# Attention of a fused two-block kernel: mask and suffix sums added onto the scores in PSUM, heads started earlier in four banks, and the convolution's taps placed at other points

## The chip, the cores and the metric

The program runs on one core of a Trainium2 chip. Its engines are TensorE (PE, matrix products, with its weight loads PEld), VectorE (DVE), ScalarE (ACT), GpSimd (POOL) and the queue SP, which issues the weight transfers. The metric is device time in microseconds, lower is better: 1041.95 us before, the median of three runs (1041.51 to 1042.3).

## The reference, cut to what matters

256 tokens of width 1024 pass through two blocks. The first (a convolution and gating mixer, 32 experts with routing, a gated projection, a final norm) isn't touched. The second begins with a norm, one wide projection `w_in_2` and three branches:

```python
h = rmsnorm_2(x, norm_mix_pre)
proj = h @ w_in                 # conv_in 1024, q 512, k 512, v 512, g_conv 1024, g_att 1024 columns
u = glu(conv_in)                                # 512 channels
u = causal_depthwise_conv(u, conv_dw_w, conv_dw_b)      # 31 taps per channel
conv_out = silu(layernorm_2(u)) @ w_conv_branch + b_conv_branch
# 8 heads of 64, two query blocks of 128:
z = einsum('bqhd,bkhd->bhqk', qb, kb) / 8
mask = s_idx < t_idx
log_1m = where(mask, log_sigmoid(-z), 0)
rev_excl = reverse_cumsum(log_1m) - log_1m
a = where(mask, exp(log_sigmoid(z) + rev_excl), 0)
att = einsum('bhqk,bkhd->bqhd', a, vb)
merged = sigmoid(g_conv) * conv_out + sigmoid(g_att) * (att @ w_att_branch)
```

A residual sum with `merged @ w_out` and a feed-forward part of width 2816 follow. Since log_sigmoid(z) equals z minus softplus(z) and log_sigmoid(-z) equals minus softplus(z), the exponent of a key s is z(s) minus the sum of softplus over all keys from s on.

## The kernel before, in words

**Data.** Tokens lie along the free axis (256 of them), channels along the 128 partitions. Each fp32 weight is used as two rounded parts: ACT writes `wh` = round(w) (`split_hi`, L259), DVE writes `wl` = w - wh (`split_lo`, L266), each in pieces of 128x1024, eight of which fit in WH and WL. Activations are in two parts as well. A product of 128 columns (`three`) is 24 matmuls of 256 columns: eight with wh and the high part, eight with wh and the low part, eight with wl. `wide` gives V with tokens on the partitions: 24 matmuls of 512 columns for each half. Piece i may be written when the product of piece i-8 is done (`freed_by`).

**Order.** It is written out by hand for each engine, and engines meet in semaphores (`Sig`): each engine runs strictly through its own list. `w_in_2` is nine groups of four pieces: group 0 and 1 the convolution's input, 2 is Q, 3 is K, 4 is V, and 5 to 8 the 16 gate products.

- `in2_pe` computes groups 0 to 4; before V two transposes (L1492) turn a row of scales into a column (`RC`).
- `in2_dve` copies products out of PSUM times the norm's scale (L1533 and L1540 for the convolution's input, L1546 for Q, L1553 for K), splits `wl`, and puts taps of the depthwise convolution between: 93 `scalar_tensor_tensor` for channel groups 0 to 2 (`taps_dve`, L1457; the first of each group is L1454). Six taps follow each Q and K copy, 13 the group of V. Eight multiplications of the residual (L1529, `x4`) stand ahead of the first copy.
- The fourth channel group is scaled by ACT (`taps_act`, L1466) and added by POOL (`att_pool`, L1689), 30 times each.
- `att_pe`, `att_dve`, `att_act` hold the attention and the 16 gate products, two gates to a head (one for head 0), in turns s = 0 to 8. For a head: `scores` (PE, two fp32 products of K and Q); DVE scales them and adds the mask into SBUF (`ZM`, L1630); ACT takes |z|, exp(-|z|) and ln(1 + .) (L1665, L1667, L1669); DVE adds max(z, 0) (L1634), which is softplus; `suffix` (PE, a triangular and an all-one matrix into another bank); DVE subtracts it from ZM (L1641); ACT takes exp (L1675); `values` (PE) multiplies with V. Scores use banks 2 and 3, suffix sums 4 and 5, values 6 and 7, gates 0 and 1. DVE copies each gate out at L1621, and the next gate but one waits for that (`sg_in`). ATH and ATL (L1681, L1647) are the two parts of the attention's output.
- `merge_*` begins with the mean over the convolution's result, which needs every tap and the last gate's copy.

Of the kernel before, what the change touches and what calls it, by code (L numbers as in the profile page):

```python
# [31 lines left out]
C_ID, C_U, C_TRI, C_NM, C_IOTA, C_IX, C_SLOT = 0, 128, 256, 384, 768, 832, 840  # L32
N_CST = 841
# [65 lines left out]
def build(nc, dr, out_ap):  # L99
    ctx = ExitStack()  # L100
    with ctx:
# [38 lines left out]
        tri = cst[:, C_TRI:C_TRI + 128]  # L140
        nm = cst[:, C_NM:C_NM + 384]
# [1265 lines left out]
        ZM = A(11384, 2, 384)  # L1407
        AB = A(o + 4608, 2, 384)
# [3 lines left out]
        TP = A(19712, 4, 256)  # L1412
        IN2 = n_piece[("in2", 0), 0]
# [11 lines left out]
        vv = sig("vv", range(2))  # L1425
        tap_v = sig("tap_v", [(3, 0)] + [(j, k) for k in range(31) for j in range(3)])
# [5 lines left out]
        s_zm = sig("zm", range(8))  # L1432
# [4 lines left out]
        s_c2 = sig("c2", range(8))  # L1437
# [30 lines left out]

        def in2_pe(e):
# [19 lines left out]
            e.wait_ge(*r45.at(0))  # L1489
            e.wait_ge(*q_.at(2))  # L1490
            for i in range(2):
                k = e.transpose(ps[2][:, i * 128:i * 128 + 128], R45[:, i * 128:i * 128 + 128], ident)  # L1492
            k.then_inc(*rcol.up("turned"))
            for i in range(2):
                wide(e, ps[i][:, :], "in2", 4, i, H5H, H5L)

        def in2_act(e):
# [12 lines left out]
            split_hi(e, IN2 + 16 + 8)  # L1510
# [4 lines left out]
            split_hi(e, IN2 + 16 + 10)  # L1515

        def in2_dve(e):
# [10 lines left out]
            for c in range(8):  # L1528
                e.tensor_tensor(XT[:, c, :], XN[:, c, :], RB[:, 1, :], M).then_inc(*x4.up(c))  # L1529
# [14 lines left out]
            for j in range(4):  # L1544
                e.wait_ge(*proj.at("in2", 2, j))
                e.tensor_tensor(QT[:, j, :], ps[j][:, 0:256], R45, M).then_inc(*q_.up(j))  # L1546
                if j == 0:
                    e.tensor_scalar(CA[:, 3, :], CU[:, 3, 0:256], dw(3, 0), vcol("dw_b", 3), M, ADD).then_inc(*tap_v.up(3, 0))
                taps_dve(e, 6)
                split_lo(e, IN2 + 8 + j + 7)  # L1550
            for j in range(4):
                e.wait_ge(*proj.at("in2", 3, j))
                e.tensor_tensor(KT[:, j, :], ps[4 + j][:, 0:256], R45, M).then_inc(*k_.up(j))  # L1553
                taps_dve(e, 6)
                split_lo(e, IN2 + 12 + j + 7)
            e.wait_ge(*rcol.at("turned"))
            e.tensor_copy(RC, ps[2][:, 0:256].rearrange("p (i n) -> p i n", i=2)[:, :, 0]).then_inc(*rc.up(0))
            split_lo(e, IN2 + 16 + 10)
            taps_dve(e, 13)

        def att_pe(e):
            def scores(h):
                b, r, j = 2 + h % 2, 64 * (h % 2), h // 2
                if h < 2:
                    e.wait_ge(*(rc.at(0) if h == 0 else q_.at(3)))
                    e.wait_ge(*k_.at(3))
                else:
                    e.wait_ge(*s_zm.at(h - 2))
                mm(e, ps[b][:, 0:256], KT[r:r + 64, j, 0:128], QT[r:r + 64, j, :], True, True)
                mm(e, ps[b][:, 256:384], KT[r:r + 64, j, 128:256], QT[r:r + 64, j, 128:256], True,  # L1570
                   True).then_inc(*s_sc.up(h))

            def suffix(h):
                b, x = 4 + h % 2, AB[:, h % 2, :]
                e.wait_ge(*s_sp.at(h))
                if h >= 2:
                    e.wait_ge(*s_c2.at(h - 2))
                mm(e, ps[b][:, 0:256], tri, x[:, 0:256], True, False)
                mm(e, ps[b][:, 128:256], one, x[:, 256:384], False, True)
                mm(e, ps[b][:, 256:384], tri, x[:, 256:384], True, True).then_inc(*s_suf.up(h))  # L1580

            def values(h):
                b, r, x = 6 + (h // 2) % 2, 64 * (h % 2), AB[:, h % 2, :]
                e.wait_ge(*s_at.at(h))
                if h == 0:
                    e.wait_ge(*vv.at(1))
# [627 lines left out]
```

## Time and profile before

| | |
|---|---|
| median of three runs | 1041.95 us |
| the profiled execution | 1045.19 us, its span 1043.5 us |
| PE / DVE / ACT / POOL busy | 957.3 / 505.4 / 330.3 / 32.3 us |
| mean granted TensorE clock | 0.968 |
| stage from 642.5 to 778.9 us of the span | second block's Q, K, V, attention, gates |

Times below are microseconds from the start of the span. In a timeline row the first number is the start, the second the time that the row covers, `xN` the number of instructions merged in it, and the bracket the idle time before it and the instruction that ended it. Merged rows overlap a little with the next, so steps are read from start to start. PEclk 1.00 is 2.4 GHz and 0.50 is 1.2 GHz. An fp32 product shows as two matmul records.

### The profile page before, as it was taken

Reading aid. Unit: us, or ns where it says so; the run is one execution under the profiler, and the core shown is the slowest. Engines: PE = TensorE matmul, PEld = TensorE weight load, DVE = VectorE, ACT = ScalarE, POOL = GpSimd, SP = SyncE. Lnnn points to the kernel's source line nnn. Section 1 sums busy time; section 2 is a strip of 40 time slices with the busy share of each in tenths; the row PEclk is TensorE's granted clock in tenths of the full one; section 3 lists DMA queues with packets and bytes.
Section 4 is the critical chain, followed back from the end, with each engine's and each line's share of the span. In section 5 each row is a group of like instructions: output and inputs, shape, how many; then the busy total and the mean of one; then the engine's idle time right before and its main releaser. Section 6 shows DMA issues by size and latency. Waiting matters only on the chain.

```text
span 1043.5 us, 14199 instructions
## 1 busy us (share of the span) xinstructions
PE 957.3 (92%) x5910; PEld 681.7 (65%) x5910; DVE 505.4 (48%) x886; ACT 330.3 (32%) x523; POOL 32.3 (3%) x39
## 2 busy tenths in 40 slices
PE   5999799999999999998989799778888989999997
PEld 5997535443434444443434788768778979999885
DVE  5684513122322222222312676986777657766742
ACT  4723211101000000100001554425557645554541
POOL 1000000000000000000000000012420000000000
PEclk9999799999999999999999899988999989999999
DMA  9947699999999999999999522442422533545401
GB/s 359 409 187 291 272 376 416 421 430 430 430 430 430 431 431 429 430 430 431 430 428 428 221 81 82 162 161 81 143 100 82 193 151 105 219 162 180 184 1 40
DMA packets 23621, 289.52 MB, mean 277 GB/s; under 512 B 2560, under 2 KB 4864, under 8 KB 6016
## 3 DMA queue, kind: packets, MB, share of 16 engines
q1 hardware_dynamic: 22832, 286.98, 67.4%
q10 hardware_dynamic: 720, 1.57, 0.4%
q8 instruction: 49, 0.80, 0.3%
q14 instruction: 20, 0.16, 0.0%
HBM read 287.49 MB, written 1.05 MB: 277 GB/s over the span
## 4 chain that ended last, share of the span: by engine, by line
PE 71%; DVE 14%; ACT 6%; DMA 5%; issue 4%; SPq 0%; DVEq 0%; ACTq 0%
PE ps L270 70%; DVE wl L266 5%; DMA ring<-in_moe 4%; DVE arena L1457 3%; ACT wh L259 2%; DMA ring<-in_w_in 1%; PE ps L959 1%; ACT arena L1466 0%; DVE arena L547 0%; DVE arena L1634 0%; DVE arena L352 0%; DVE arena L1641 0%; ACT arena L1665 0%; ACT arena L1669 0%; ACT arena L1667 0%
## 5 line engine op out<-in xcount | busy, mean ns | idle before, releaser
L270 PE MATMUL ps<-ring,arena 128*64 128x512 f32 x1232 | 341.5, 598 | 8.6 <-issue 8.5
L270 PEld LDWEIGHTS ps<-ring,arena 128*64 128x64 f32 x1232 | 109.5, 138 | 170.1 <-issue 167.9
L266 DVE TENSOR_TENSOR wl<-ring,wh 128x1024 fp32r<-128x1024 f32 x150 | 180.2, 1231 | 63.3 <-ACT wh L259 63.2
L270 PE MATMUL ps<-arena 128*64 128x512 f32 (+5 forms) x432 | 163.3, 533 | 13.2 <-ACT arena L1675 11.6
L259 ACT ACTIVATE wh<-ring 128x1024 fp32r<-128x1024 f32 x150 | 150.8, 1049 | 33.1 <-PE ps L270 29.7
L1070 DVE SCALAR_TENSOR_TENSOR arena<-ps,arena 128x512 f32<-128x512 f32 x16 | 12.0, 750 | 216.5 <-PE ps L270 216.5
L270 PEld LDWEIGHTS ps<-arena 128*64 128x64 f32 (+2 forms) x432 | 59.1, 149 | 61.4 <-issue 44.3
L270 PE MATMUL ps<-up_h,wh 128*128 128x256 f32 x352 | 88.3, 286 | 4.6 <-DVE up_l L1866 4.6
L270 PE MATMUL ps<-up_l,wh 128*128 128x256 f32 x352 | 87.8, 285 | 0.0
L270 PE MATMUL ps<-h_h,wh 128*128 128x256 f32 x256 | 69.2, 302 | 5.0 <-DVE wl L266 2.5
L270 PEld LDWEIGHTS ps<-up_h,wh 128*128 128x128 f32 x352 | 67.5, 192 | 4.9 <-issue 4.9
L1143 ACT ACTIVATE y_h<-ps 128x512 fp32r<-128x512 f32 x32 | 19.1, 597 | 158.5 <-PE ps L270 158.5
L270 PEld LDWEIGHTS ps<-up_l,wh 128*128 128x128 f32 x352 | 67.5, 192 | 0.0
L270 PE MATMUL ps<-h_l,wh 128*128 128x256 f32 x256 | 66.9, 293 | 0.0
L1084 DVE TENSOR_TENSOR arena<-arena,ps 128x512 f32<-128x512 f32 x64 | 40.9, 680 | 41.7 <-PE ps L270 41.7
L270 PEld LDWEIGHTS ps<-h_h,wh 128*128 128x128 f32 x256 | 51.2, 200 | 6.9 <-issue 4.1
L270 PE MATMUL ps<-up_h,wl 128*128 128x256 f32 x352 | 54.7, 285 | 0.0
L270 PEld LDWEIGHTS ps<-h_l,wh 128*128 128x128 f32 x256 | 51.2, 200 | 0.0
L1076 DVE TENSOR_TENSOR y_l<-ps,y_h 128x512 fp32r<-128x512 f32 x32 | 22.0, 687 | 59.2 <-ACT y_h L1143 59.2
L1136 ACT ACTIVATE arena<-ps 128x512 f32<-128x512 f32 x16 | 9.6, 597 | 128.4 <-PE ps L959 128.4
L1689 POOL TENSOR_TENSOR arena<-arena 128x256 f32<-128x256 f32 x30 | 27.3, 910 | 718.5 <-ACT arena L1466 716.1
L270 PEld LDWEIGHTS ps<-up_h,wl 128*128 128x128 f32 x352 | 48.0, 192 | 0.0
(260 smaller groups left out, 1531.1 us busy)
## 6 DMA issues: line engine op xcount, KB each, us to landing
ring<-in_moe SPq DMA_DIRECT2D x77, 2048.0 KB, 22.1
arena<-in_moe SPq DMA_DIRECT2D x19, 2048.0 KB, 26.6
ring<-in_w_in SPq DMA_DIRECT2D x12, 2048.0 KB, 8.8
ring<-in_w_up SPq DMA_DIRECT2D x11, 2048.0 KB, 7.7
ring<-in_w_dn SPq DMA_DIRECT2D x5, 2048.0 KB, 7.8
ring<-in_w_out SPq DMA_DIRECT2D x4, 2048.0 KB, 14.9
ring<-in_w_pg SPq DMA_DIRECT2D x2, 2048.0 KB, 21.5
ring<-in_w_in SPq DMA_DIRECT2D x2, 1024.0 KB, 10.4
```

Of the source, the lines that this page charges most:

```text
L259: e.activation(wh(i), raw_piece(i), ACT.Copy).then_inc(*hi.up(i))
L266: e.tensor_tensor(wl(i), raw_piece(i), wh(i), SUB).then_inc(*lo.up(i))
L270: return e.matmul(o, l, r, start=first, stop=final, skip_group_check=True)
L959: k = e.transpose(ps[4][:, f * 128:f * 128 + 128], HD[:, f * 128:f * 128 + 128], ident)
L1070: e.scalar_tensor_tensor(out=HD, in0=ps[1][:, :], scalar=RW[:, q % 2, 1:2], in1=HD, op0=M, op1=M).then_inc(*hid.up(q))
L1076: e.tensor_tensor(l[:, :], ps[5 + n][:, :], h[:, :], SUB).then_inc(*yl.up(q, n))
L1084: e.tensor_tensor(x, x, ps[ZB[z]][:, :], ADD).then_inc(*acc.up(q, z))
L1136: e.activation(HT.rearrange("p a b -> p (a b)"), ps[4][:, :], ACT.Copy).then_inc(*b4.up(q))
L1143: e.activation(parted(q, n)[0][:, :], ps[5 + n][:, :], ACT.Copy).then_inc(*yh.up(q, n))
L1457: e.scalar_tensor_tensor(out=CA[:, j, :], in0=src, scalar=dw(j, k), in1=CA[:, j, :], op0=M, op1=ADD).then_inc(*tap_v.up(j, k))
L1689: e.tensor_tensor(CA[:, 3, :], CA[:, 3, :], TP[:, k % 4, :], ADD).then_inc(*tap_p.up(k))
```

## The change

**Scores.** Q is scaled by 0.125 when it is copied out. The mask is added on PE: a product of the identity and the mask, both rounded (`IDR`, `NMR`, two new ACT copies), goes onto the scores' bank, once for each masked square, two per head. ACT reads |z| from PSUM. `suffix` multiplies with -1 matrices and accumulates onto the same bank, and ACT's last exp reads PSUM. L1630 and L1641, eight instructions each on DVE, are gone, and so is ZM. A head keeps one of the banks 2 to 5 from its scores to its last exp, and one of four AB buffers.

**Order.** Heads 0 to 3 get their scores within groups 3 and 4, heads 0 and 1 their suffix sums too; the rest stand one by one between the gates. ACT takes softplus of heads 0 to 3 and exp of 0 and 1 in `in2_act`. The eight residual multiplications go behind group 4's splits. Taps: three for each Q copy and for each K copy but the last, and behind the split; 12 around the first heads; four for each of the first 15 gates. ACT's taps begin during Q, where its splits for pieces 14 on now wait behind `tap_v` (3, 0), DVE's first instruction on channel group 3.

The core of the diff (ACT's and DVE's parts of a head become the helpers `softplus_act`, `softplus_dve` and `weights_act`):

```diff
+        def scores(e, h):
+            b, r, j = 2 + h % 4, 64 * (h % 2), h // 2
+            e.wait_ge(*k_.at(j))
+            if h == 0:
+                for x in range(2):
+                    e.wait_ge(*masks.at(x))
+            elif h == 2:
+                e.wait_ge(*rc.at(0))
+            elif h >= 4:
+                e.wait_ge(*s_at.at(h - 4))
+            mm(e, ps[b][:, 0:256], KT[r:r + 64, j, 0:128], QT[r:r + 64, j, :], True, False)
+            mm(e, ps[b][:, 0:128], IDR[:, :], NMR[:, :], False, False)
+            mm(e, ps[b][:, 256:384], KT[r:r + 64, j, 128:256], QT[r:r + 64, j, 128:256], False, False)
+            mm(e, ps[b][:, 256:384], IDR[:, :], NMR[:, :], False, False).then_inc(*s_sc.up(h))
...
 in2_pe:
+                if j in (1, 2):
+                    scores(e, j - 1)
...
+            suffix(e, 0)
+            wide(e, ps[0][:, :], "in2", 4, 0, H5H, H5L)
+            suffix(e, 1)
+            scores(e, 2)
+            wide(e, ps[1][:, :], "in2", 4, 1, H5H, H5L)
+            scores(e, 3)
...
 in2_act:
+            e.wait_ge(*tap_v.at(3, 0))
+            for j in range(8):
+                split_hi(e, IN2 + 15 + j)
+                taps_act(e, 1)
+                if j == 6:
+                    softplus_act(e, 0)
+            softplus_act(e, 1)
...
 in2_dve:
             split_lo(e, IN2 + 10)
-            for c in range(8):
-                e.tensor_tensor(XT[:, c, :], XN[:, c, :], RB[:, 1, :], M).then_inc(*x4.up(c))
...
-                taps_dve(e, 6)
                 split_lo(e, IN2 + 8 + j + 7)
+                taps_dve(e, 3)
...
+            softplus_dve(e, 0)
...
 att_pe:
+            for g in range(16):
...
+                if g in (1, 3, 5, 7):
+                    scores(e, 4 + g // 2)
+                if g in (0, 2, 4, 6, 8, 10):
+                    suffix(e, 2 + g // 2)
+                if g in (0, 1, 2, 4, 6, 8, 10, 12):
+                    values(e, (0, 1, 2, 4, 6, 8, 10, 12).index(g))
```

DVE's list around Q and the first K copy, before (`proj`: the product is done; `hi`: the piece of wh is there):

```order
L1546 TENSOR_TENSOR arena<-ps1,arena 128x256 [waits proj]
L1457 SCALAR_TENSOR_TENSOR arena<-arena,vec 128x256 [waits tap_v] x6
L266 TENSOR_TENSOR wl_51<-ring,wh_50 128x1024 [waits hi]
L1546 TENSOR_TENSOR arena<-ps2,arena 128x256 [waits proj]
L1457 SCALAR_TENSOR_TENSOR arena<-arena,vec 128x256 [waits tap_v] x6
```

The same place in the changed kernel, to the first K copy (L1625 copies Q, L1453 and L1456 are taps, L1633 copies K):

```order
L1625 SCALAR_TENSOR_TENSOR arena<-ps0,arena 128x256 [waits proj,cpad,glu]
L1628 TENSOR_SCALAR arena<-arena,vec 128x256
L266 TENSOR_TENSOR wl_51<-ring,wh_50 128x1024 [waits hi]
L1453 TENSOR_SCALAR arena<-arena,vec 128x256 x3
L1625 SCALAR_TENSOR_TENSOR arena<-ps1,arena 128x256 [waits proj]
L266 TENSOR_TENSOR wl_51<-ring,wh_50 128x1024 [waits hi]
L1456 SCALAR_TENSOR_TENSOR arena<-arena,vec 128x256 [waits tap_v] x3
L1625 SCALAR_TENSOR_TENSOR arena<-ps2,arena 128x256 [waits proj]
```

Three taps stand where six stood, behind the split and not ahead of it.

PE's list in group 3 in the changed kernel, with what is added there (`+`) between the second and the third K product:

```order
 L270 MATMUL ps5<-h5_h_65,wl_51 128x256 x7
+L270 MATMUL ps2<-arena 128x256 [waits masks,k]
+L270 MATMUL ps2<-nm_r_70,id_r_69 128x128
+L270 MATMUL ps2<-arena 128x128
+L270 MATMUL ps2<-nm_r_70,id_r_69 128x128
 L270 MATMUL ps6<-h5_h_65,wh_50 128x256 [waits hi,glu]
```

Head 0's scores wait for the first K copy, and the third K product, which needed only `hi` and `glu`, now stands behind that wait.

DVE's list between two gates, before:

```order
L1641 TENSOR_TENSOR arena<-arena,ps5 128x384 [waits suffix]
L1457 SCALAR_TENSOR_TENSOR arena<-arena,vec 128x256 [waits tap_v] x2
L1621 TENSOR_TENSOR arena<-ps0,arena 128x256 [waits proj]
L266 TENSOR_TENSOR wl_51<-ring,wh_50 128x1024 [waits hi]
L1457 SCALAR_TENSOR_TENSOR arena<-arena,vec 128x256 [waits tap_v] x2
L1630 SCALAR_TENSOR_TENSOR arena<-ps2,cst 128x384 [waits c2,scores]
```

and in the changed kernel (L1669 copies a gate, L1519 is the softplus sum of a head):

```order
L1669 TENSOR_TENSOR arena<-ps1,arena 128x256 [waits proj]
L266 TENSOR_TENSOR wl_51<-ring,wh_50 128x1024 [waits hi]
L1456 SCALAR_TENSOR_TENSOR arena<-arena,vec 128x256 [waits tap_v] x4
L1519 SCALAR_TENSOR_TENSOR arena<-ps2,arena 128x384 [waits ln]
L1669 TENSOR_TENSOR arena<-ps0,arena 128x256 [waits proj]
```

Both DVE steps that waited for a head's products are gone from between the gates, and a gate has four taps there.

## Rows read from the trace of the kernel before

**Rows 1.** Which engines were busy (the page, part 1; share of the span)

```profile
PE 957.3 (92%) x5910; PEld 681.7 (65%) x5910; DVE 505.4 (48%) x886; ACT 330.3 (32%) x523; POOL 32.3 (3%) x39
```

**Rows 2.** Busy time, PEclk, DMA share and GB/s in three stretches, all engines

```profile
642.50:668.00 25.50, 23.20 (x193) 23.02 (x194) 22.03 (x47) 15.74 (x18) 0.00 (x0) 1.00 0.47 167
668.00:701.10 33.10, 21.21 (x107) 17.35 (x105) 30.04 (x61) 6.62 (x10) 0.24 (x1) 0.89 0.43 164
701.10:778.90 77.80, 66.23 (x441) 59.76 (x441) 55.73 (x88) 42.49 (x77) 27.05 (x30) 0.92 0.30 109
```

**Rows 3.** Who PE waited for from 640 to 780 (total, times, longest)

```profile
PE ps L270 <- ACT arena L1675: 11.6, 7, 2.8
PE ps L270 <- DVE wl L266: 7.5, 1, 7.5
PE ps L270 <- DVE arena L1634: 4.4, 1, 4.4
PE ps L270 <- DVE arena L1533: 1.6, 1, 1.6
PE ps L270 <- ACT wh L259: 0.7, 1, 0.7
```

**Rows 4.** PE's timeline: V, a head with a gate, the stage's end

```profile
679.58 3.75 PE L270 MATMUL ps<-wl,h_h 128*128 128x512 f32 x8 [7.55 <-DVE wl L266]
...
683.13 0.48 PE L270 MATMUL ps<-wh,h_h 128*128 128x512 f32 x1
...
688.91 0.92 PE L270 MATMUL ps<-arena 64*128 64x256 f32 x4
...
741.76 1.71 PE L270 MATMUL ps<-arena 128*64 128x256 f32 x8 [1.80 <-ACT arena L1675]
...
743.41 0.39 PE L270 MATMUL ps<-h_h,wh 128*128 128x256 f32 x1
...
746.36 0.59 PE L270 MATMUL ps<-arena,cst 128*128 128x256 f32 x2
...
747.16 0.37 PE L270 MATMUL ps<-h_h,wh 128*128 128x256 f32 x1
...
752.04 1.71 PE L270 MATMUL ps<-arena 128*64 128x256 f32 x8 [1.79 <-ACT arena L1675]
...
778.87 1.99 PE L270 MATMUL ps<-arena,ones 128*128 128x256 f32 x8
```

**Rows 5.** DVE's timeline: residual, first Q copy, six taps, a split

```profile
640.97 2.76 DVE L1529 TENSOR_TENSOR arena<-arena 128x256 f32<-128x256 f32 x8
...
656.19 0.42 DVE L1546 TENSOR_TENSOR arena<-ps,arena 128x256 f32<-128x256 f32 x1
...
660.48 2.45 DVE L1457 SCALAR_TENSOR_TENSOR arena<-arena,vec 128x256 f32<-128x256 f32 x6
...
662.85 1.21 DVE L266 TENSOR_TENSOR wl<-ring,wh 128x1024 fp32r<-128x1024 f32 x1
...
663.99 0.41 DVE L1546 TENSOR_TENSOR arena<-ps,arena 128x256 f32<-128x256 f32 x1
```

**Rows 6.** ACT's timeline: ten splits, and one step of softplus

```profile
649.55 9.60 ACT L259 ACTIVATE wh<-ring 128x1024 fp32r<-128x1024 f32 x10
...
747.13 0.53 ACT L1665 ACTIVATE arena<-arena 128x384 f32<-128x384 f32 x1 [2.60 <-DVE arena L1630]
```

**Rows 7.** PE alone in short stretches: busy, PEclk, DMA share, GB/s

```profile
672.00:676.00 4.00, 0.04 (x1) 1.00 0.00 0
680.00:683.00 3.00, 3.00 (x8) 0.50 0.91 279
711.00:717.00 6.00, 6.00 (x23) 0.50 0.77 317
```

**Rows 8.** Timelines of DVE (two taps) and POOL (four additions)

```profile
734.51 1.83 DVE L1457 SCALAR_TENSOR_TENSOR arena<-arena,vec 128x256 f32<-128x256 f32 x2
731.90 4.16 POOL L1689 TENSOR_TENSOR arena<-arena 128x256 f32<-128x256 f32 x4 [6.12 <-ACT arena L1466]
```

More of the change, by code:

```diff
@@ L1412, in build @@
         TP = A(19712, 4, 256)
+        IDR, NMR = rounded("id_r", 20736, 128), rounded("nm_r", 20864, 128)
         IN2 = n_piece[("in2", 0), 0]
@@ L1469, in in2_pe, with weights_act @@
+        def weights_act(e, h):
+            e.wait_ge(*s_suf.at(h))
+            e.activation(AB[h % 4], ps[2 + h % 4][:, 0:384], ACT.Exp).then_inc(*s_at.up(h))
         def in2_pe(e):
@@ L1599, in gates @@
                 three(e, ps[j % 2][:, 0:256], "in2", 5 + n, j, H5H, H5L)
-            for s in range(9):
-                if s < 8:
-                    scores(s)
-                if 1 <= s < 8:
-                    gates()
-                if s >= 1:
-                    suffix(s - 1)
-                gates()
-                if s >= 1:
-                    values(s - 1)
+                if g in (1, 3, 5, 7):
+                    scores(e, 4 + g // 2)
+                if g in (0, 2, 4, 6, 8, 10):
+                    suffix(e, 2 + g // 2)
@@ new lines, in rest @@
+            def rest(j):
+                e.wait_ge(*at_h.at(j))
+                e.tensor_tensor(ATL[:, j, :], ps[6 + j % 2][:, 0:256], ATH[:, j, :], SUB).then_inc(*at_l.up(j))
+            for g in range(16):
+                if g:
+                    gate(g - 1)
+                split_lo(e, IN2 + 20 + g + 7)
+                if g in (3, 6, 10, 14):
+                    rest((3, 6, 10, 14).index(g))
+                if g == 0:
+                    softplus_dve(e, 3)
+                taps_dve(e, 4)
+                if g in (2, 4, 6, 8):
+                    softplus_dve(e, 3 + g // 2)
@@ new lines, in rounded_part @@
+            def rounded_part(j):
+                e.wait_ge(*s_val.at(2 * j + 1))
+                e.activation(ATH[:, j, :], ps[6 + j % 2][:, 0:256], ACT.Copy).then_inc(*at_h.up(j))
+            for g in range(16):
+                if g in (1, 3, 5, 7, 9, 11):
+                    weights_act(e, 2 + g // 2)
+                if g in (2, 4, 6, 8):
+                    softplus_act(e, 3 + g // 2)
+                if g in (2, 5, 9, 13):
+                    rounded_part((2, 5, 9, 13).index(g))
+                split_hi(e, IN2 + 20 + g + 7)
+                taps_act(e, 1)
```

186 lines of the change are left out of this document (72 added, 114 removed).

## Prediction

> **What bounds the kernel now.** I read the page first. PE is busy 92% of the span [rows 1], and a change to it that saves no matmuls can pay only where PE waits or runs slowly. Second, the busy time by stretch [rows 2]: in the stage that the change touches, from 642.5 to 778.9, PE is busy 110.6 of 136.4 us, by a measure that counts slow matmuls as busy, and the granted clock is below full in the last two stretches (0.89, 0.92). DVE is busy 22.0 of 25.5, then 30.0 of 33.1, then 55.7 of 77.8 us. So DVE is nearly full until the heads begin and has room after that. Third, PE's waits [rows 3]: 7.5 us for the low parts of V's weights, 4.4 for the first softplus, 11.6 in seven waits for a head's last exp, 1.6 for the first copy behind the residual's products, and 0.7 for a split. Last, the timelines, for the steps of a turn.
>
> The steady turn is one head and two gates. It takes 752.04 - 741.76 = 10.28 us [rows 4]. Of it PE needs 1.65 for values and the next scores (741.76 to 743.41), 2.95 from there to the next suffix sum, 0.80 for that (746.36 to 747.16), and some 2.9 for the other gate: 8.2 to 8.3, and 1.8 is the wait. I use 2.85 for a product of 24 matmuls (0.119 each), 0.83 each for scores and values, 0.80 for suffix sums. Half of V takes 688.91 - 683.13 = 5.78. The wait ends a ring through DVE and ACT: mask, three ACT steps of 0.53 [rows 6], sum, suffix sums, subtraction, exp. DVE's own work does not fill a turn.
>
> **The change part by part.** All in the time of the profiled execution (1045.19 us, 3.2 above the median of the runs shown).
>
> *Residual moved.* Eight DVE products, 2.7 us [rows 5], leave the head of the copies. What follows on DVE and ACT (copies, sigmoids, splits) is 2.7 earlier: the first Q copy at 656.19 - 2.7 = 653.5. PE's waits of 1.6 and 0.7 go.
>
> *When PE reaches head 0's scores.* PE began its long wait at 679.58 - 7.55 = 672.0, after 16 matmuls of V (3.9) and two short transposes: group 3 ended near 668.0. Less 2.3 it is 665.7, and the second K product, two products earlier, ends at 660.0.
>
> *When DVE gives it K.* Between the first Q copy and the end of the first K copy DVE has four Q copies (0.35 to 0.41, so 1.5), one scaling (0.4), four splits of 663.99 - 662.85 = 1.14 (4.6), twelve taps of 2.37 / 6 = 0.395 (4.7) and the K copy (0.35): 11.6 us. Two things come on top. ACT's splits now stand behind `tap_v`; ACT is free of it at 654.3, a split takes 0.96 [rows 6], and DVE waits 1.0. Queued behind that wait on ACT are all later splits, which it then makes at 1.4 with a tap each, faster than DVE uses them. And POOL's additions now begin during Q, six of them by then. Beside two additions two taps take 1.83 instead of 0.79 [rows 8], 0.5 for each addition: 3.0. Bounds: nothing, if they fall on instructions that POOL does not disturb; POOL's whole 27.05 / 30 = 0.9 [rows 2], so 5.4. I take 0.5, the row for the same pair of operations. Sum 15.6: K is there at 669.1, and **PE waits 9 us** where it waited 7.5 later on. This is the price of the early scores: products 3 and 4 of K queue behind them. The clock goes low in such a wait: it did in the wait of 7.5 us, and was at 1.2 GHz until 683 after PE resumed at 679.6 [rows 4, 7]. I charge 1.8 us, half of that time.
>
> *To the first gate.* Mask products: 16 in all, of 128 columns, not in this trace. Not above 0.20 (a quarter of a suffix sum, by fp32 columns), not below nothing; nearest is a rounded matmul of 256 columns, 0.119, and I take 0.12, so 1.07 for scores. From 669.1: scores, K, scores, K (7.8) and 1.8 for the clock, 678.7. DVE then needs the last K copy, a split and the softplus sum (2.0): suffix sums start at 680.7. Suffix, V, suffix, scores, V, scores: 0.8 + 5.8 + 0.8 + 1.1 + 5.8 + 1.1 = 15.3, and the first gate starts at 696.0. The low parts of V have long been split by then, so the wait of 7.5 goes, and so does the one of 4.4.
>
> *The gates.* PE: 16 x 2.85 + 6 x 0.80 + 8 x 0.83 + 4 x 1.07 = 61.3, ending at 757.3 if nothing holds it. DVE: 18 splits (20.5), 60 taps (23.7), 17 additions of POOL beside it (8.5), 16 copies (5.9), five softplus sums and four low parts (4.0, at about 0.45, between a copy and ACT's 0.53): 62.6. It can begin when ACT has done softplus of head 3 (1.6) and a split (1.0) after PE's 696.0, at 698.6, so it ends at 761.2. The two run within 4 us of each other over 16 gates, and each gate has about one gate's time of slack (a gate waits for the copy two before). Exp, softplus and splits on ACT are some 2.5 us a gate, with room; a head's exp is a gate ahead of its values, so the 11.6 us go. Taps are not removed anywhere: DVE loses 16 instructions of 384 columns (8.5 us at ACT's 0.53 for the same size), and takes on nearly as much by POOL's additions, of which four began 2.6 us before DVE's pair of taps in [rows 8] and now find DVE at work. That is why DVE, and not PE, ends the stage.
>
> *The sum.* The mean over the convolution starts at 761.2 and not at 778.87 [rows 4]: -17.7 us. What follows has the same instructions and the same order, and weights are no limit: transfers take 0.47, 0.43 and 0.30 of these stretches [rows 2]. 1045.19 - 17.7 = 1027.5, against the median 1041.95 - 17.7 = **1024.3**.
>
> On POOL and DVE the trace shows 0.5 us lost by DVE for an addition. The Trainium skill, SBUF — State Buffer, section "SBUF: two separate sides", says that the port pair they share is an exclusive lock, and that the loser is blocked for the whole instruction. The sum above goes by the row; by the rule, with DVE always the loser, it would be the third case below. The row agrees in kind, since both engines slow down (POOL 1.04 an addition in [rows 8]), and not in that size.
>
> **The rivals.**
>
> *PE ends the stage (additions cost DVE little).* Then K comes 3.0 earlier, the first gate starts at 693.0, PE ends at 754.3 and the last copy at 754.7: -24.2, 1017.8. For it: splits and PSUM copies may be undisturbed, and they are a third of DVE's time. Against it: 1.83 for two taps.
>
> *DVE pays 0.9 for each addition.* 6 x 0.4 more before K and 17 x 0.4 in the gates: 9.2, which leaves -8.5, 1033.5. For it: DVE has almost no idle time now for POOL to run in. Against it: no row has DVE paying in full.
>
> *The heads don't run ahead.* If one in-order queue still ties each head's exp to the gate before it, two gates keep 10.28: 696.0 + 8 x 10.28 = 778.2, no change, 1041.3. For it: ACT waits in order for suffix sums ahead of splits. Against it: softplus of heads 0 to 3 is done before the first gate.
>
> *Slower: the clock stays low.* The mechanism is the wait for K: if PE goes to 1.2 GHz there and further waits keep it there through the gates, a gate with its part of the heads, 61.3 / 16 = 3.83 at full clock, takes up to twice that; V's last eight matmuls show 3.55 / 8 = 0.44 for 512 columns at the low level (679.58 to 683.13 [rows 4]) against 0.24, so 1.8 times, 3.05 more a gate. PE may end 778.87 - 757.3 = 21.6 later before the gain is gone: that is seven gates. With all 16 it is 48.8 - 21.6 = 27 later than before, 1069. For it: in this trace the clock was low again from 711 to 717. Against it: that followed waits of 4.4 and 2.8 us close together, and later waits of 1.8 in every turn left it at 2.4 GHz; the gates should have none above 1.
>
> **How the numbers follow.** The forecast 0.60, with 1018 to 1030 as its own range; PE ends the stage 0.15; additions in full 0.13; no running ahead 0.07; clock low 0.05. The time is that of the forecast, 1024. The range takes in the second and third case: 1014 to 1034. A change under 0.2% (2.1 us) can't be told from none here. Faster is the first three and a part of the fourth, 0.90; same 0.05; slower 0.05.
>
> **What would show it.** PE waits about 9 us between the second and the third K product, for K's copy, with the clock low for 3 to 4 us after it; a wait near 2 before head 0's suffix sums; no wait for V's low parts; from the first gate to the mean some 65 us, DVE busy over 90% of it, and taps there at 0.5 or more on average; PE's waits in the gates for the copy of a gate and not for exp. I am wrong if PE waits in the gates for exp or suffix sums, if the clock falls there, or if the part after the attention changes in length by more than 2 us.

## The result, and the profile after

| | before | after |
|---|---|---|
| median of the runs side by side | 1041.73 us (1040.66 to 1042.3) | 1030.09 us (1027.85 to 1033.81) |
| the profiled execution / its span | 1045.19 / 1043.5 us | 1029.13 / 1027.4 us |
| mean granted clock | 0.968 | 0.973 |

The ratio is 0.9893, with a 95% interval of 0.9861 to 0.9925: the change is faster by 1.1%, which is clear of the noise but less than 2%. The forecast was 1024, its range 1014 to 1034.

The two profiled executions differ by 16.1 us, more than the medians do. About 5 us of that belong to neither order of the attention: in the profile of before the stage begins at 630.80, in that of after at 625.85, and what stands ahead of it (the first block) is the same code. Over the fourteen profiles of this study that start lies anywhere between 625.9 and 630.8. So I measure the **stage**: from DVE's first reciprocal of the second norm to PE's first product of the mean over the convolution. It holds all that the change touches. Waits inside it repeat to 0.01 us between kernels that share the code up to them, and what follows it takes 263.5 to 265.8 us in every profile. What doesn't repeat is where TensorE's clock is low behind a wait; the section on the experiments says what that comes to.

| | start | mean starts | stage | rest |
|---|---|---|---|---|
| before | 630.80 | 778.87 | 148.07 | 264.6 |
| after | 625.85 | 762.66 | 136.81 | 264.7 |

The stage is 11.3 us shorter; 17.7 were forecast. 11.3 agrees with the medians (11.6).

The page of after, part 1, answers to [rows 1]. PE's share of the span rose by a point, since the same products and the 16 for the mask stand in less time:

```profile
PE 955.8 (93%) x5926; PEld 679.4 (66%) x5926; DVE 499.5 (49%) x870; ACT 329.9 (32%) x525; POOL 37.8 (4%) x39
```

Busy time in three stretches of after (columns as in [rows 2]): to the end of the wait for K, from there to the first gate, and from the first gate to the mean:

```profile
637.50:663.70 26.20, 17.25 (x145) 16.95 (x143) 22.09 (x38) 15.98 (x23) 5.30 (x6) 0.88 0.54 208
663.70:694.10 30.40, 28.49 (x134) 22.91 (x135) 22.10 (x42) 12.61 (x23) 9.03 (x7) 0.88 0.38 139
694.10:762.60 68.50, 65.79 (x477) 58.86 (x477) 59.97 (x103) 37.17 (x61) 18.31 (x17) 1.00 0.33 123
```

The reader is to see where PE now has holes: 9 us in the first stretch, 1.9 in the second, 2.7 in the last. In the last one PE is busy 65.79 of 68.5 us at full clock, while DVE is busy 59.97, but that isn't spread evenly. DVE alone over the last 27.6 us of the stage, and two rows of its timeline there:

```profile
735.00:762.60 27.60, 27.60 (x47) 1.00 0.40 153
```

```profile
753.82 3.60 DVE L1456 SCALAR_TENSOR_TENSOR arena<-arena,vec 128x256 f32<-128x256 f32 x4
757.34 0.41 DVE L1669 TENSOR_TENSOR arena<-ps,arena 128x256 f32<-128x256 f32 x1
```

DVE has no hole there; four taps took 3.60 us beside four of POOL's additions, where 1.66 is usual. PE's last two waits (1.03 at 757.81 and 1.74 at 762.66) are for its copies of gates. Who PE waited for from 636 to 766 in after answers to [rows 3]:

```profile
PE ps L270 <- DVE arena L1633: 9.0, 1, 9.0
PE ps L270 <- DVE arena L1669: 2.8, 2, 1.7
PE ps L270 <- DVE arena L1519: 1.9, 1, 1.9
```

The waits of 11.6, 7.5, 4.4, 1.6 and 0.7 us are gone, 25.8 in all, and 13.7 took their place. The timeline of PE in after shows the three places, and two steps of a turn:

```profile
663.71 1.22 PE L270 MATMUL ps<-arena 64*128 64x256 f32 x2 [8.96 <-DVE arena L1633]
...
677.91 1.14 PE L270 MATMUL ps<-arena,cst 128*128 128x256 f32 x6 [1.90 <-DVE arena L1519]
...
685.44 0.70 PE L270 MATMUL ps<-arena 64*128 64x256 f32 x2
...
686.07 0.33 PE L270 MATMUL ps<-nm_r,id_r 128*128 128x128 f32 x1
...
686.33 0.48 PE L270 MATMUL ps<-arena 64*128 64x128 f32 x2
...
686.74 0.33 PE L270 MATMUL ps<-nm_r,id_r 128*128 128x128 f32 x1
...
686.90 0.45 PE L270 MATMUL ps<-wh,h_h 128*128 128x512 f32 x1
...
694.11 0.33 PE L270 MATMUL ps<-h_h,wh 128*128 128x256 f32 x1
...
708.91 0.39 PE L270 MATMUL ps<-h_h,wh 128*128 128x256 f32 x1
...
718.08 0.39 PE L270 MATMUL ps<-h_h,wh 128*128 128x256 f32 x1
```

A head's scores with its two mask products take 686.90 - 685.44 = 1.46 us. Two gates with one head take 718.08 - 708.91 = 9.17, where they took 10.28 [rows 4]. PE alone behind the wait for K (busy, PEclk, DMA share, GB/s) answers to [rows 7]:

```profile
664.00:671.00 7.00, 7.00 (x29) 0.51 0.40 122
672.00:676.00 4.00, 4.00 (x30) 1.00 0.49 209
```

Through 7 us of unbroken work the granted clock is 1.2 GHz, and 2.4 GHz from 670.8 on, 7.1 us after PE resumed. DVE's timeline around the first Q copy and the K copy, which answers to [rows 5]:

```profile
648.56 0.42 DVE L1625 SCALAR_TENSOR_TENSOR arena<-ps,arena 128x256 f32<-128x256 f32 x1
...
653.30 1.69 DVE L266 TENSOR_TENSOR wl<-ring,wh 128x1024 fp32r<-128x1024 f32 x1
...
654.91 2.21 DVE L1456 SCALAR_TENSOR_TENSOR arena<-arena,vec 128x256 f32<-128x256 f32 x3
...
662.06 1.26 DVE L1456 SCALAR_TENSOR_TENSOR arena<-arena,vec 128x256 f32<-128x256 f32 x3
663.25 0.41 DVE L1633 TENSOR_TENSOR arena<-ps,arena 128x256 f32<-128x256 f32 x1
```

Three taps take 1.26 us alone and 2.21 beside POOL's additions, a split 1.69 instead of 1.21.

### The profile page after: what moved, and what is told of

It reads as the page before. It is cut to its first block, busy times and chain, and to the rows that moved or that the text cites. A ratio compares the mean times of both kernels' runs of the same rounds, so it can differ in the third digit from the quotient of the medians.

```text
span 1027.4 us, 14198 instructions
## 1 busy us (share of the span) xinstructions
PE 955.8 (93%) x5926; PEld 679.4 (66%) x5926; DVE 499.5 (49%) x870; ACT 329.9 (32%) x525; POOL 37.8 (4%) x39
## 4 chain that ended last, share of the span: by engine, by line
PE 77%; DVE 11%; DMA 4%; ACT 4%; issue 3%; SPq 0%; DVEq 0%; ACTq 0%
PE ps L270 76%; DVE wl L266 4%; DMA arena<-in_moe 4%; DVE arena L1456 2%; ACT wh L259 1%; PE ps L959 1%; DMA vec<-in_vec 0%; DVE arena L547 0%; DVE arena L352 0%; ACT arena L1762 0%; ACT in_h L617 0%; DVE arena L1084 0%; DVE arena L1669 0%; DVE arena L1805 0%; ACT arena L1765 0%
## 5 line engine op out<-in xcount | busy, mean ns | idle before, releaser
L270 PE MATMUL ps<-arena 128*64 128x512 f32 (+4 forms) x432 | 163.9, 530 | 10.6 <-DVE arena L1633 9.0
L1709 POOL TENSOR_TENSOR arena<-arena 128x256 f32<-128x256 f32 x30 | 32.6, 1088 | 695.8 <-ACT arena L1465 694.7
```

The costliest lines, as they stand in the source:

```text
L270: return e.matmul(o, l, r, start=first, stop=final, skip_group_check=True)
L1709: e.tensor_tensor(CA[:, 3, :], CA[:, 3, :], TP[:, k % 4, :], ADD).then_inc(*tap_p.up(k))
```

## Experiments

I compare by the stage, since the medians carry the changing start as well. The ratio is against before.

| kernel | median us (lowest to highest) | ratio, 95% interval | stage |
|---|---|---|---|
| after | 1030.09 (1027.85 to 1033.81) | 0.9893, 0.9861 to 0.9925 | 136.81 |
| sums_only | 1027.77 (1026.7 to 1030.43) | 0.9868, 0.9849 to 0.9887 | 134.18 |
| warm | 1028.77 (1026.44 to 1032.34) | 0.9886, 0.9861 to 0.991 | 133.71 |
| q_taps_later | 1025.76 (1022.11 to 1027.9) | 0.9839, 0.9817 to 0.9861 | 131.86 |
| mask_out | 1026.83 (1025.08 to 1027.97) | 0.9861, 0.9841 to 0.9881 | 131.02 |
| mask_one | 1026.22 (1025.29 to 1027.98) | 0.9868, 0.9849 to 0.9887 | 132.24 |
| mask_twice | 1027.08 (1024.5 to 1028.36) | 0.985, 0.9818 to 0.9881 | 132.87 |
| split_first | 1028.59 (1026.12 to 1031.04) | 0.9885, 0.9864 to 0.9905 | 137.27 |
| act_taps_later | 1027.81 (1027.18 to 1028.26) | 0.9851, 0.9815 to 0.9887 | 134.15 |
| residual_back | 1034.77 (1032.38 to 1035.24) | 0.9914, 0.9886 to 0.9942 | 141.50 |
| best1 | 1020.09 (1017.59 to 1021.06) | 0.9793, 0.9776 to 0.981 | 126.90 |
| old_order_tuned | 1015.4 (1013.8 to 1017.98) | 0.9754, 0.9737 to 0.9771 | 119.71 |
| old_order_tuned2 | 1013.87 (1013.55 to 1014.28) | 0.9719, 0.9689 to 0.9749 | 120.31 |

Each stage is read from one profile, and the clock in it varies. Here the stage of the kernels in the new order is cut at head 0's scores (K is there) and at the first gate. The fifth column is PE's work at 1.2 GHz behind the wait for K; the last says whether the clock fell again behind the wait of 1.90 us for head 0's softplus sum, which all ten have.

| kernel | K there | K to first gate | first gate to mean | low clock behind K | falls again |
|---|---|---|---|---|---|
| after | 37.86 | 30.40 | 68.55 | 7.1 | no |
| warm | 37.89 | 27.28 | 68.54 | none | no |
| q_taps_later | 31.52 | 31.84 | 68.50 | 6.8 | yes |
| mask_out | 37.86 | 26.97 | 66.19 | 4.5 | no |
| mask_one | 37.86 | 27.69 | 66.69 | 4.8 | no |
| mask_twice | 37.85 | 27.74 | 67.28 | 3.9 | no |
| split_first | 37.87 | 32.33 | 67.07 | 7.9 | yes |
| act_taps_later | 35.11 | 30.50 | 68.54 | 7.3 | no |
| residual_back | 40.54 | 32.42 | 68.54 | 8.1 | yes |
| best1 | 31.54 | 30.17 | 65.19 | 6.7 | yes |

The lists of after and split_first are the same up to head 0's suffix sums, and yet the clock fell behind the wait of 1.90 in one and not in the other. A row of PE's timeline and PE alone in split_first, to set beside the row at 677.91 above, which took 1.14:

```profile
680.33 1.90 PE L270 MATMUL ps<-arena,cst 128*128 128x256 f32 x6 [1.90 <-DVE arena L1519]
```

```profile
680.00:683.00 3.00, 2.67 (x9) 0.59 0.00 0
```

That second fall, with a longer first one, puts the first gate 1.93 us later. So a difference of up to 2 us between two stages, if it lies between K and the first gate, is not the edit's. Why the clock fell in one execution and not in the other is open.

### sums_only: the new sums in the old order

Before, with one part of the change alone: mask and suffix sums accumulate on the scores' bank. Two banks, the old turns, all taps and the residual stay where they were.

```diff
-                mm(e, ps[b][:, 0:256], KT[...], QT[...], True, True)
-                mm(e, ps[b][:, 256:384], KT[...], QT[...], True, True).then_inc(*s_sc.up(h))
+                mm(e, ps[b][:, 0:256], KT[...], QT[...], True, False)
+                mm(e, ps[b][:, 0:128], IDR[:, :], NMR[:, :], False, False)
+                mm(e, ps[b][:, 256:384], KT[...], QT[...], False, False)
+                mm(e, ps[b][:, 256:384], IDR[:, :], NMR[:, :], False, False).then_inc(*s_sc.up(h))
...
-                b, x = 4 + h % 2, AB[:, h % 2, :]
+                b, x = 2 + h % 2, AB[:, h % 2, :]
```

> The kernel before with the arithmetic of the change alone: the mask added by the identity product and the suffix sums accumulated onto the scores in PSUM, in the old order, the old two banks, and with the old places of the taps and the residual. Theory: a turn of one head and two gates (10.28 us before) is a ring, and the ring loses two DVE steps on either side of ACT (0.5 + 0.5 us) while PE gains two mask products (0.6), so a turn takes 9.6 to 10.0 and the whole -2 to -5 us against before (about 1038). V's wait of 7.5 us stays. Rival (the order alone brings the gain, the arithmetic nothing): 1041 to 1042. Rival (the arithmetic brings most of it): 1033 or less.

Measured: stage 134.18, so -13.9 from before, 2.6 better than the whole change. What I expected failed by 8.9 us at least, and the rival that gave the arithmetic most of the gain (1033 or less) held: 1027.77. PE's waits from 636 to 766 in this kernel:

```profile
PE ps L270 <- DVE wl L266: 7.5, 1, 7.5
PE ps L270 <- DVE arena L1633: 2.3, 1, 2.3
PE ps L270 <- DVE arena L1536: 1.7, 1, 1.7
PE ps L270 <- ACT wh L259: 0.7, 1, 0.7
```

There is no wait for an exp: the 11.6 us of [rows 3] are gone without any head running ahead. A turn, read on DVE's softplus sums of two heads, is 726.55 - 717.58 = 8.97 us:

```profile
717.58 0.56 DVE L1633 SCALAR_TENSOR_TENSOR arena<-ps,arena 128x384 f32<-128x384 f32 x1 [0.45 <-ACT arena L1664]
...
726.55 0.56 DVE L1633 SCALAR_TENSOR_TENSOR arena<-ps,arena 128x384 f32<-128x384 f32 x1 [1.05 <-ACT arena L1664]
```

PE alone from 700 to 720, in before and then in sums_only:

```profile
700.00:720.00 20.00, 16.06 (x75) 0.66 0.29 105
```

```profile
700.00:720.00 20.00, 20.00 (x138) 0.93 0.28 106
```

So a part of the gain is the clock. Before worked 16.6 us at 1.2 GHz, behind its waits of 7.5, 4.4 and 2.8; sums_only 7.1, behind 7.5 and 2.3. By the price that warm shows below (3.1 for 7.1 us) the 9.5 us are worth some 4, an estimate, and PE's waits fell by 13.6; the mask products take some 4.5 of it back.

So the arithmetic carries the gain. The new order as a whole added nothing to it: it swapped V's wait of 7.5 for K's of 9.0, and its stage is 2.6 longer. Whether it really costs that much isn't shown, with one profile of each and run times that overlap (1026.7 to 1030.43 against 1027.85 to 1033.81).

### warm: PE kept at work in the wait for K

72 products into an unused bank, of operands that are there, ahead of head 0's scores. Nothing waits for them.

```diff
+                if j == 1:
+                    e.wait_ge(*glu.at(3))
+                    for _ in range(72):
+                        mm(e, ps[7][:, 0:256], H5H[:, 0, 0:128], H5H[:, 0, :], True, True)
                 if j in (1, 2):
                     scores(e, j - 1)
```

> The changed kernel with 72 idle matmuls of 256 columns (their output is never read) put on PE between the second K product and head 0's scores, where it waits 9 us for K. They should end about when K comes. Theory: the wait costs a second time through the clock, which stayed at 1.2 GHz for 7.7 us after it; with PE kept busy the clock stays at 2.4 GHz and the time falls by 3 to 4 us, less what DVE then holds back, so -2 to -4 against the changed kernel (about 1027), and its runs agree within 1 us of each other where they spread over 6. Rival (DVE sets the end, the clock costs nothing): 1030, no change. Rival (the spread of 6 us comes from elsewhere): the spread stays.

Measured: stage -3.1. PE's timeline, then PE alone in two stretches (columns as in [rows 7]):

```profile
655.29 8.79 PE L270 MATMUL ps<-h_h 128*128 128x256 f32 x72
664.43 0.70 PE L270 MATMUL ps<-arena 64*128 64x256 f32 x2 [0.35 <-DVE arena L1637]
```

```profile
658.00:664.00 6.00, 6.00 (x51) 1.00 0.67 284
664.00:671.00 7.00, 6.65 (x43) 1.00 0.27 75
```

43 matmuls in the 7 us in which after made 29. The low clock behind the wait costs 3.1 us, not the 1.8 that I charged. (It lasted 7.1 us in after; the 7.7 that I expected from was misread.) The spread of the run times stayed at 6 us, where I had expected 1, so the clock in this place is not what makes the runs differ.

### q_taps_later: the taps between the Q copies moved behind the group

```diff
                 split_lo(e, IN2 + 8 + j + 7)
-                taps_dve(e, 3)
...
             split_lo(e, IN2 + 24)
+            taps_dve(e, 6)
             for c in range(8):
...
-            taps_dve(e, 6)
+            taps_dve(e, 12)
```

> The changed kernel with the 12 taps between Q's copies put behind the softplus sums of heads 0 and 1 (6 more before the residual, 6 more after it). Theory: the wait for K is DVE's queue, so K comes 12 x 0.4 + 1.5 to 3 us of POOL's contention earlier, the wait falls from 9 to 2 or 3 us and the clock stays up; the first gate starts 9 to 10 us earlier, DVE does the taps partly in its idle time of 3.7 and 2.9 us, and the whole is 5 to 9 us faster than the changed kernel: 1021 to 1025. Rival (DVE's total work bounds the stage): -1 to -3, 1027 to 1029. Rival (wait is for something else): 1030.

Measured: stage -5.0, and K's wait is 2.62 instead of 8.96:

```profile
661.47 0.70 PE L270 MATMUL ps<-arena 64*128 64x256 f32 x2 [2.62 <-DVE arena L1632]
```

The wait shrank by 6.3 and the stage by 5.0, the low end of what I expected; the difference is the clock, which I had expected to stay up. K to the first gate took 31.84 instead of 30.40. PE alone in this kernel:

```profile
658.00:661.00 3.00, 0.85 (x8) 1.00 0.78 224
663.00:668.00 5.00, 5.00 (x24) 0.50 0.47 161
671.00:674.00 3.00, 2.63 (x23) 1.00 0.56 240
676.00:678.00 2.00, 2.00 (x8) 0.50 0.00 0
```

The clock fell after a wait of 2.6 us as it had after 9, here at 662.1, 0.6 us after PE had resumed, and once more behind the wait of 1.9 for head 0's softplus sum. A wait's price is its length and a period at 1.2 GHz. That period doesn't go by the wait's length: it was 6.8 us of work here, and 3.9 to 8.1 behind the same wait of 9 in the table above.

### mask_out, mask_one, mask_twice: what the mask products cost

mask_out leaves out the mask products, and with them the causal mask:

```diff
-            mm(e, ps[b][:, 0:128], IDR[:, :], NMR[:, :], False, False)
             mm(e, ps[b][:, 256:384], KT[...], QT[...], False, False)
-            mm(e, ps[b][:, 256:384], IDR[:, :], NMR[:, :], False, False)
```

> The changed kernel without the 16 mask products: the causal mask is left out of the attention. Theory: scores took 1.46 us a head with them against 0.83 before, so the mask costs 0.4 to 0.6 a head on PE, and PE sets the pace of the first eight gates; four heads of it lie ahead of the first gate, so the first gate comes 1.6 to 2.4 earlier and the whole is 2 to 4 us faster than the changed kernel: 1026 to 1028. Rival (my estimate of the prediction, 0.24 a head): -1, 1029. Rival (DVE bounds the gates): -1 to -2.

mask_one holds the mask twice (one more ACT copy) and adds it by one product of 256 columns, to columns 0 to 127 and 256 to 383 at once, behind both score products:

```diff
-            mm(e, ps[b][:, 0:128], IDR[:, :], NMR[:, :], False, False)
             mm(e, ps[b][:, 256:384], KT[...], QT[...], False, False)
-            mm(e, ps[b][:, 256:384], IDR[:, :], NMR[:, :], False, False)
+            mm(e, ps[b][:, 0:384].rearrange("p (a n) -> p a n", a=3)[:, 0:3:2, :], IDR[:, :], NMR[:, :, :],
+               False, False)
```

> The changed kernel with one mask product a head (both masked squares in one matmul of 256 columns) in place of two. I judge by the stage, from the reciprocal ahead of the residual to the mean over the convolution, since the part before it varies by 5 us between executions: 136.8 us in the changed kernel, 131.0 without any mask. Theory: what costs is the product as such (0.31 us each by the starts, of which few are columns), so half of it goes: stage 134 to 135, time -2 to -3 (1027 to 1028). Rival (columns cost): no change.

mask_twice is mask_one with this product issued twice in a row, so that the mask is added twice.

> The kernel with one mask product of 256 columns a head, but that product issued twice (the mask is added twice, which changes no weight of the attention). It tells why two products of 128 columns cost 0.62 us a head and one of 256 costs 0.13. Theory (a rounded product of 128 columns is slow as such): a second one of 256 adds 0.12 a head, the stage is 132.2 + 1 = 133 to 133.5, time 1027. Rival (a second rounded product among the fp32 ones costs, whatever its columns): 136 to 137, 1030.

Measured: stage -5.8 without the mask (I had expected 2 to 4), -4.6 with one product of 256 columns (expected 2 to 3), and +0.6 for that product again. The gates' first matmuls two gates apart, in mask_out, mask_one and mask_twice:

```profile
706.73 0.39 PE L270 MATMUL ps<-h_h,wh 128*128 128x256 f32 x1
...
715.34 0.39 PE L270 MATMUL ps<-h_h,wh 128*128 128x256 f32 x1
```

```profile
706.97 0.39 PE L270 MATMUL ps<-h_h,wh 128*128 128x256 f32 x1
...
715.69 0.39 PE L270 MATMUL ps<-h_h,wh 128*128 128x256 f32 x1
```

```profile
706.40 0.39 PE L270 MATMUL ps<-h_h,wh 128*128 128x256 f32 x1
...
715.29 0.39 PE L270 MATMUL ps<-h_h,wh 128*128 128x256 f32 x1
```

A turn is 8.61 us without a mask, 8.72 with one product of 256 columns, 8.89 with two of them in a row, and 9.17 in after with two of 128 columns, one of which stands between two fp32 products. So the two narrow products cost 0.56 a turn and the wide one 0.11. I had 0.24. Eight heads at 0.56 are 4.5 us. The other 1.3 of the 5.8 lies between K and the first gate, where mask_out also worked 4.5 us at the low clock and after 7.1; by the price from warm that is 1.2, an estimate, and no effect of the mask that is shown. The rows of after above show where the 0.56 lies: 0.26 for the first mask product and 0.16 for the second, and the score products around them take 0.63 + 0.41, where they take 0.84 in mask_out:

```profile
685.12 0.92 PE L270 MATMUL ps<-arena 64*128 64x256 f32 x4
...
685.96 0.50 PE L270 MATMUL ps<-wh,h_h 128*128 128x512 f32 x1
```

The number of products doesn't explain it (two wide ones in a row cost half as much). The edit from after to mask_one changed two things at once, the width of the product and the switch from fp32 to rounded operands and back in the middle of the scores. Two narrow products behind both score products would tell them apart; that wasn't tried.

### split_first: ACT's splits ahead of its softplus

DVE waited in the gates of after for ACT's splits, which stand behind softplus in ACT's queue. Row of DVE's waits from 694 to 766 in after:

```profile
DVE wl L266 <- ACT wh L259: 8.7, 4, 2.9
```

```diff
                 if g in (1, 3, 5, 7, 9, 11):
                     weights_act(e, 2 + g // 2)
+                split_hi(e, IN2 + 20 + g + 7)
                 if g in (2, 4, 6, 8):
                     softplus_act(e, 3 + g // 2)
...
-                split_hi(e, IN2 + 20 + g + 7)
```

> The changed kernel with ACT's weight split ahead of softplus in gates 2, 4, 6 and 8, and one split ahead of softplus of head 3. Theory: DVE's waits of 2.9, 2.0, 1.7 and 2.0 us for splits stand behind ACT's wait for scores; without them DVE keeps up, PE's last waits (2.8 us for gate copies) and the chain through DVE from 732 on go, and the stage is 2.5 to 4 shorter than 136.8 (133 to 134), the time 1026 to 1028. Rival (PE sets the gates, DVE's waits cost nothing): 136 to 137, 1030.

Measured: stage +0.5. But that sum hides two things. The first gate came 1.94 us later, by the second fall of the clock shown above, which the edit doesn't reach. From there to the mean the stage took 67.07 instead of 68.55: DVE's waits fell to 7.2 and the longest from 2.9 to 1.9, PE's waits for a gate's copy went from two (2.8) to one of 1.6. So the edit gained 1.5 us, less than the 2.5 to 4 that I expected, and DVE's waits for splits in the gates are not all slack. best1 below has it again: 65.19 with this edit, 66.69 in mask_one without it.

### act_taps_later: no additions by POOL beside Q and K

```diff
                 split_hi(e, IN2 + 15 + j)
-                taps_act(e, 1)
...
             split_hi(e, IN2 + 24)
-            taps_act(e, 3)
+            taps_act(e, 7)
```

The four others moved go behind head 2's softplus.

> The changed kernel with ACT's seven taps, and so POOL's additions, moved out of the Q and K loops to behind V's halves. Theory: six additions beside DVE cost 2.7 us ahead of K; without them K comes 2.7 earlier and PE's wait is 6.3, the clock still falls; later additions cost DVE the same where it has idle time: stage 134 to 135, time 1028. Rival (additions cost the same wherever they stand): 136 to 137, 1030.

Measured: stage -2.7, K's wait 6.2 instead of 9.0, as expected. Six additions of POOL cost DVE 2.7 us here, 0.45 each.

### residual_back: the eight residual products at the head of the copies again

```diff
             split_lo(e, IN2 + 10)
+            for c in range(8):
+                e.tensor_tensor(XT[:, c, :], XN[:, c, :], RB[:, 1, :], M).then_inc(*x4.up(c))
             e.wait_ge(*r45.at(0))
```

> The changed kernel with the residual's eight products back at their old place, ahead of the first copy. Theory: the whole chain of DVE up to K is 2.7 us later and PE waits for K a little longer than 9 (its own wait of 1.6 returns): stage 136.8 + 2 to 2.7 = 139 to 139.5, time 1032 to 1033. Rival (it falls into DVE's idle 3.7 us at heads 2, where it now stands, at both places): no change, 1030.

Measured: stage +4.7. The first copies are 2.7 later and PE's waits of 1.7 and 0.7 are back. K is 2.7 later, and the other 2.0 lie between K and the first gate: the first low period was longer, and the suffix sums of head 0 and the products behind them ran at the low clock again (1.81 us for the suffix sums instead of 1.14). split_first shows the same 2 us with the residual where it is in after. So what is shown for the residual is its own 2.7 us.

### best1: the three edits together

q_taps_later, mask_one and split_first in one kernel.

> The three edits on the changed kernel together: taps of the Q loop later, one mask product, split ahead of softplus. If they add up, the stage is 131.9 - 2 - 3 = 127 and the time 1020 to 1022. If DVE's total work bounds it once the waits are gone: 129 to 130, 1024.

Measured: stage 126.90, -9.9 from after, as expected. By parts, with K's arrival (-6.3), the mask (-4.6) and the splits (-1.5 in the gates), it should have been -12.4. K came 6.3 earlier and the gates took 3.4 less, about the 1.9 of mask_one and the 1.5 of split_first. Between K and the first gate it took 30.17 where mask_one took 27.69: its low clock behind K lasted longer, and the clock fell again.

### old_order_tuned and old_order_tuned2: fewer taps ahead of the copies, in the old order

If the arithmetic carries the gain, the old order should be the one to tune. sums_only with mask_one's product, the residual behind K, and the taps evened out:

```diff
-                taps_dve(e, 6)          # behind each Q and K copy
+                taps_dve(e, 3)
-            taps_dve(e, 13)             # behind V's splits
+            taps_dve(e, 5)
-                taps_dve(e, 2)          # in a turn, ahead of the gates
+                taps_dve(e, 4)
-                taps_dve(e, 2)          # behind them
+                taps_dve(e, 3)
```

> The old order with the new arithmetic (stage 134.2 in that kernel) and three further edits: three taps for each Q and K copy where six stood, 5 behind V where 13 stood and 4 and 3 where 2 and 2 stood between the gates; the residual behind K; one mask product. Theory: the early heads are not needed at all. V's wait of 7.5 us and the low clock after it go (-9), the residual's -1.7, the masks' -2: stage 121 to 123, 1015 to 1018. Rival (DVE, with 7 taps a turn and 8.8 us of work, sets the turn and gives part back): 125 to 127, 1019 to 1021, and then still not worse than the early heads with the same edits.

Measured: 1015.4 us, stage 119.71, 17.1 below after and 14.5 below sums_only, more than I expected. The edits were made at once, and which of them brings how much was not taken apart. In old_order_tuned2 two more taps stand behind each of the last two K copies:

```diff
-                taps_dve(e, 3)
+                taps_dve(e, 3 if j < 2 else 5)
```

> The old order with the new arithmetic, tuned as before, with five taps and not three behind the last two K copies, where DVE then waited 3 us for splits; the gates' last turn has fewer taps. Theory: the mean's wait of 2.4 us for the last taps falls to under 1, stage 118 to 119 against 119.7, time 1013 to 1015. Rival (the taps make head 0's softplus late by as much): 119.7, 1015.

Measured: 1013.87 us, stage 120.31. PE's waits from 636 to 766, and 120 us of the stage (columns as in [rows 2]), in old_order_tuned2:

```profile
PE ps L270 <- DVE arena L1633: 2.3, 1, 2.3
PE ps L270 <- DVE arena L1626: 0.8, 1, 0.8
PE ps L270 <- DVE wl L266: 0.4, 1, 0.4
```

```profile
628.00:748.00 120.00, 116.44 (x839) 107.39 (x837) 114.39 (x192) 70.64 (x113) 25.96 (x30) 0.99 0.43 158
```

I had expected 118 to 119. The wait for the last taps at the end (2.4 us in old_order_tuned) went, and one of 2.3 for head 0's softplus came where 0.7 had been, as the rival said. The period of low clock moved too: behind the mean, outside the stage, in old_order_tuned, and inside it here. Stage and rest together are 385.6 and 384.9, so the two kernels are about the same. PE is busy 97% of the 120 us at a clock of 0.99 and DVE 95%: both are near their end in this stage. This kernel beats before by 2.8% and after by 1.6% (1013.87 against 1030.09). That the old order is the better one isn't shown by it, since the new order was never given the same taps.

## Why the forecast was right in sign and 6 us too low

Measured from the stage's start, since in the profiles it lies 4.95 apart.

| step | forecast | measured |
|---|---|---|
| first Q copy | 22.7 | 22.71 |
| end of the second K product | 29.2 | 28.9 |
| K there, head 0's scores | 38.3 | 37.86 |
| PE's wait for K | 9 | 8.96 |
| low clock behind it | 3 to 4 us, costs 1.8 | 7.1 us, costs 3.1 |
| wait for head 0's softplus sum | 2.0 | 1.90 |
| first gate | 65.2 | 68.26 |
| first gate to the mean | 65.2 | 68.55 |
| a head and two gates | 8.4 | 9.17 |

The 6.4 us are 0.4 less up to K, 3.5 more from there to the first gate, and 3.35 more in the gates.

**Up to the scores** every term held, POOL's price on DVE among them: 0.5 for an addition was taken from a pair of taps [rows 8], and act_taps_later gives 0.45. The rule of the Trainium skill that I set beside it (SBUF — State Buffer, section "SBUF: two separate sides": the loser of the shared port is blocked for the whole instruction) would, with DVE always the loser, make it lose all of an addition each time. The runs agree in kind, not in that size: 0.45 of at least 0.73. The case with 0.9 an addition is out.

**The mask products** are the first term that was mis-sized. The prediction had "nearest is a rounded matmul of 256 columns, 0.119, and I take 0.12", 1.9 us in all. The turns show 0.56 a head, 4.5 in all: 2.6 of the 6.4 us that are missing. The upper bound of 0.20 for one didn't hold either: it priced the columns of the new product, and not what it does to the fp32 products on both sides.

**The clock** took 1.3 more. I had read the low period from [rows 7], where the row at 0.50 ends 3.4 us after PE resumed (the clock came back at 683.3, after 3.7), and took half of it; here it lasted 7.1. As the table of the experiments shows, that length is partly luck.

**The gates.** The prediction had PE done in 61.3 us and DVE, which starts 2.6 later and needs 62.6, ending the stage at 65.2. Neither came out so. PE's own work was 4.5 more, 65.8 of the 68.55 us. A turn shows where, 9.17 instead of 8.40: 0.39 in the scores with their masks, 0.24 in the two gates (I used 2.85 for one, though [rows 4] has 2.95), 0.17 in the suffix sums (0.97 instead of 0.80), and 0.03 less in values. DVE's own work was less than I had, 59.97 (88% of the stretch and not over 90%; a tap took 0.48 and not 0.5 or more). But it also waited 8.7 us for ACT's splits, which stand behind softplus in ACT's queue. 2.9 of that is the wait at the start, which the prediction had at 2.6; the other 5.7 it put at nothing ("with room"). So DVE fell behind: from 735.0 on it had no hole, and PE lost 2.8 us to its last copies. "DVE, and not PE, ends the stage" is right for the last two gates, and by these waits, not by the sum. PE sets the pace of the others. split_first takes 1.5 of the 3.35 us away.

Between K and the first gate some 0.9 of the 3.5 us stay open, beside 1.3 for the clock and 1.3 for four heads' masks.

**Which part of the change pays** was wrong, and no number of the forecast showed it. The step "a head's exp is a gate ahead of its values, so the 11.6 us go" credits them to the order. sums_only has them gone in the old order. The ring that ends the wait held two steps in DVE's queue, the mask and the subtraction, and each of them also waited its turn behind taps, a copy and a split; without them it fits into a turn. That is read from the two lists of DVE; no run takes away one of the two steps alone. The long low periods behind the waits of before went with them. What then is left of the order is an exchange: the residual moved (worth 2.7 by K in residual_back), V's wait of 7.5 and the low clock behind it gone, and K's wait of 9.0 with 3.1 of low clock come in. The time could not show the error, since both parts came together.

Of the rivals, "PE ends the stage" is out as it was put, since additions do cost DVE 0.45 and PE's own work was longer than its 1017.8 allowed; "the heads don't run ahead" is out, and so is the clock that stays low through the gates (1.00 there). The part after the stage kept its length, as it had to.

## What to carry to other kernels

When a change joins new arithmetic with a new order, price each alone: the ring that got shorter may fit into the old order already. In an in-order queue, count for each engine what stands ahead of the instruction that another engine waits for, and move the work that nobody needs yet (taps here) behind it: with the moved residual and one mask product that took 14.5 us off the stage of sums_only, where the whole change had taken 11.3 off before. When stages of single profiles are compared, cut them where the edit begins and look at the granted clock ahead of it; here the clock made 2.0 of residual_back's 4.7 us, and in split_first it turned a gain of 1.5 into a loss of 0.5. A small product that goes between others on PE is priced by the turn with and without it, not by its columns.

## What the runs showed of the hardware that I had not expected

- Two rounded products of 128 columns added to a head's fp32 scores cost 0.56 us a turn, one of 256 columns 0.11. Whether the width or the switch of type costs it is open.
- The granted clock fell to 1.2 GHz behind a wait of 2.6 us in q_taps_later as behind 9 us in after, and behind the same wait of 1.90 us in four kernels and not in the six others. It stayed low for 3.9 to 8.1 us of unbroken work behind the wait for K, and cost 0 or about 2 us more between K and the first gate with the same lists. 72 products that nobody reads kept it at 2.4 GHz and gave 3.1 us back.
- An addition on POOL (0.73 us where DVE is idle at 669.5, 0.73 to 1.37 beside DVE) costs DVE 0.45 us.
